# A hybrid residual layer in fp32 on one core: the opening sweep in seven stages, and GpSimd's exponent of its own

## The chip, the cores and the metric

The kernel runs on one core of a Trainium2 chip. The metric is the device time of one execution, in microseconds. Engines: TensorE (PE) multiplies matrices, VectorE (DVE) and ScalarE (ACT) work on elements, GpSimd (POOL) does small sums and issues some loads, and SyncE (SP) issues nearly all loads.

## The reference, cut to what matters

One layer over a sequence of 256 tokens of width 2048, all in fp32: an adaptive norm, a token mixer with one input projection, an output projection, a second norm, and a mixture of 32 experts. What the change touches is the head of it.

```python
ada = silu(c) @ w_ada + b_ada                     # w_ada: 2048 x 12288
sh_m, sc_m, gt_m, sh_f, sc_f, gt_f = split(ada, 6)
h = rms_norm(x, g_pre_mix) * (1 + sc_m) + sh_m    # x: 256 x 2048
proj = h @ w_in                                   # w_in: 2048 x 6160
...
x = x + gt_m * rms_norm(y, g_post_mix)
h = rms_norm(x, g_pre_ffn) * (1 + sc_f) + sh_f
y = hier_moe(h, ...)                              # 32 experts, w1, w3, w2
x = x + gt_f * rms_norm(y, g_post_ffn)
```

## The kernel before

The width of 2048 is 16 chunks of 128 columns. To project chunk k of h, the kernel needs 128 columns of the shift and of the scale, and each of these is a product of silu(c) with 2048 rows of w_ada. The opening sweep does both side by side, in stages of a few chunks. STAGES says which chunks are in which stage: before, six stages of 2, 3, 3, 3, 3 and 2.

**Loads.** SyncE's queue loads for each stage first its columns of w_ada, in pieces (4 rows to a partition for a stage of two chunks, 2 rows for one of three, `rows_of`), for shift and scale separately. One row of a piece is 128 columns times the chunks of the stage, which is 1,024 bytes for two chunks and 1,536 for three. A chunk of w_ada is 2.10 MB in all. Eight pieces fit in; for the ninth SyncE waits until the first is used up (`piece_done`). Then it loads the stage's rows of w_in, 2,560 columns (8,192 bytes and 2,048 bytes a row, 1.31 MB a chunk). There are homes for 8 chunks of w_in, so a stage's load waits until the stage is over (`stage_ps`) that used the home before. Behind the sweep stand the first two further units of w_in, 4 MB each, which wait for the last pieces, and the other columns of w_ada.

**VectorE.** `early(j)` multiplies and adds the sixteen rows of w_ada of stage j (L1208 for the first, L1210 for the others), transposes (L1221) and reduces (L1223) into `sums`. Between the pieces it also makes the additions of the stage before. TensorE has ten units of output columns to do in a stage, in the order of TURN. Six are held in PSUM banks over all stages. The other four, units 6 to 9, share one bank: when TensorE has ended one, VectorE adds it to its home (`added`, L1193 in the first stage, L1196 later), and only then may TensorE start the next of the four. ADDED_AT says behind which piece each addition comes, and unit 9's comes after the reduction:

```python
TURN = [6, 0, 7, 1, 8, 2, 3, 4, 9, 5]
ADDED_AT = {8: {1: 6, 3: 7, 5: 8}, 4: {0: 6, 2: 7, 3: 8}}   # pieces in a stage: {piece: unit}
...
if j and n_ in ADDED_AT[len(pieces(j))]:
    added(j - 1, ADDED_AT[len(pieces(j))][n_])
```

So VectorE is a stage ahead of TensorE: while TensorE does stage j, VectorE does the rows of stage j+1 and the additions of stage j.

**TensorE.** It first transposes x by two diagonal matrices of the inverse norms (L681). Before the ninth unit of a stage it folds the next stage's sums (L687), which needs them finished. The units' matmuls are at L717 (units 0 to 7) and L710 (units 8 and 9, against 512 columns). ScalarE takes the folded sums, forms shift and scale of each chunk (L1729, L1730) and applies them to the transposed x (L1734); the next stage's first unit waits for that.

**The first norms.** ScalarE squares both halves of x (L1714), GpSimd turns the sums into inverse roots (`rms`, L1976 and a power at L1979), and ScalarE makes the diagonals (L1719). The power's exponent, -0.5, is a column of the constants, whose second part (323 KB) is loaded last on ScalarE's queue; GpSimd waits for that part (`const_in[1]`).

Behind the sweep come two blocks of the projection, the other units with attention beside them, the output projection, routing, and the experts, whose weights are loaded into a ring of five places as matmuls free them.

Of the kernel before, what the change touches and what calls it, by code (L numbers as in the profile page):

```python
# [26 lines left out]
D = 2048  # L27
# [24 lines left out]
C_ID, C_LT, C_SUF, C_ONE, C_IOTA, C_NH, C_HALF, C_FOLD, C_FLIP, C_PAIR, C_BKT = 0, 128, 256, 384, 512, 544, 548, 550, 582, 710, 774  # L52
# [9 lines left out]
FIN_DVE = [(0, 0), (0, 1), (1, 0), (1, 1), (1, 2)]  # L62
FIN_PE = [(0, 2), (0, 3), (1, 3)]
X1T_BANK = [[2, 3, 4, 5], [6, 7, 0, 1]]
STAGES = [(0, 2), (2, 5), (5, 8), (8, 11), (11, 14), (14, 16)]
HOMES = 8
EARLY = 8
WIDE = 10
# [12 lines left out]

def rows_of(j):

    return {2: 4, 3: 2, 4: 2}[STAGES[j][1] - STAGES[j][0]]


def pieces(j):

    before = sum(KD // rows_of(i) for i in range(j))
    return [(before + i, rows_of(j) * i, rows_of(j) * (i + 1)) for i in range(KD // rows_of(j))]  # L90


PIECES = sum(KD // rows_of(j) for j in range(len(STAGES)))
HALF_PIECE = 2 * len(range(0, PIECES, 8)) + 1


def stage_of(k):

    return [lo <= k < hi for lo, hi in STAGES].index(True)


def slabs(j):

    lo, hi = STAGES[j]
    half = HOMES // 2
# [4 lines left out]
def wide_slabs(j):  # L110

    lo, hi = STAGES[j]
    cuts = [lo] + [k for k in range(lo + 1, hi) if k % HOMES in (0, 6)] + [hi]
# [106 lines left out]
def loads():  # L220

    out = [(4 * i + 3.9, ("unit", i + 3)) for i in range(7)]
    out += [(max(ada_slot(n - 4) + 0.5, 1.9), ("ada", n)) for n in range(4, 64)]
    return [("unit", 1), ("unit", 2), ("ada", 0), ("ada", 1), ("ada", 2), ("ada", 3)] + [item for _, item in sorted(out)]


def build(nc, a, out):
    f32, i32, u32 = mybir.dt.float32, mybir.dt.int32, mybir.dt.uint32
    ALU, ACT, AX = mybir.AluOpType, mybir.ActivationFunctionType, mybir.AxisListType
    SCHED = schedule()  # L230
    ctx = ExitStack()
    with ctx:
        def sb(name, shape, dt=f32):
            return ctx.enter_context(nc.sbuf_tensor(name, shape, dt))

        def sem(name):
            return ctx.enter_context(nc.semaphore(name))
# [9 lines left out]
        cst = sb("cst", [P, C_KEEP])  # L247
# [9 lines left out]
        st = sb("st", [P, 84])  # L257
# [126 lines left out]
        def piece(j, c):  # L384

            n = P * (STAGES[j][1] - STAGES[j][0])
            lo = UNIT // 4 * (c % 4)
# [3 lines left out]
        def unit_w(i):  # L391

            return slab(S1 if i % 2 else S0, 0, KD, 512)
# [23 lines left out]
        def ada_quarter(n):  # L417

            q = (n + 2) % 4
            return S2[:, D * q:D * q + D]  # L420
# [5 lines left out]
        c_in, tab_in, const_in, x_in, par_in, late_in = sem("c_in"), sem("tab_in"), [sem("const_in0"), sem("const_in1")], [sem("x_in0"), sem("x_in1")], sem("par_in"), sem("late_in")  # L426
        bias_in, rel_out = sem("bias_in"), sem("rel_out")
        unit_in = [sem(f"unit_in{i}") for i in range(2)]
        piece_in, piece_done = [sem(f"piece_in{n}") for n in range(8)], sem("piece_done")
# [6 lines left out]
        act_c, dve_c, pool_c = sem("act_chain"), sem("dve_chain"), sem("pool_chain")  # L436
        relrow_ps, relrow_sb = sem("relrow_ps"), sem("relrow_sb")
        small_exp, scale_sb = sem("small_exp"), sem("scale_sb")
        xsq, xr = sem("xsq"), sem("xr")
# [97 lines left out]
        def _(sp):  # L537
# [15 lines left out]
            for kind, i in loads():  # L553
                if kind == "unit":
                    if i == 1:
                        sp.wait_ge(piece_done, PIECES)
                    elif i == 2:
                        sp.wait_ge(piece_done, PIECES - 4)
                    elif i in (3, 4):
                        sp.wait_ge(blk_ps, 7 * (i - 2))  # L560
                    else:
                        sp.wait_ge(proj_ps, HELD + 2 * (i - 4))
                    if i < 8:
                        c = ORDER[4 + i]
                        sp.dma_start(unit_w(i), w_in[:, :, 512 * c:512 * c + 512]).then_inc(unit_in[i % 2], 16)
                    else:
                        u = i - 8
                        sp.dma_start(unit_w(i), w_out[:, :, 512 * u:512 * u + 512]).then_inc(unit_in[i % 2], 16)
                else:
                    if i in (0, 1):  # L570
                        sp.wait_ge(stage_ps, stage_of(11) + 1)
                    elif i >= 4:
                        sp.wait_ge(ada_done, i - 3)
                    sp.dma_start(ada_quarter(i), w_ada[:, i % KD, 2 + i // KD, :]).then_inc(ada_in[i % 4], 16)

            def first_load(n, w, js=(0, 1)):
                for j in js:
                    sp.dma_start(half(ring(n), j), half(w, j)).then_inc(ring_in[n % RING][j], 16)

            sp.wait_ge(ada_done, 64)  # L580
            sp.wait_ge(unit_in[1], 16 * 6)
            sp.wait_ge(piece_in[0], 16 * HALF_PIECE)
            first_load(1, w3[0])
# [87 lines left out]
        def _(pe):  # L671
# [72 lines left out]
            for item in SCHED:  # L744
# [11 lines left out]
                elif kind == "alpha":  # L756
# [12 lines left out]
                    else:  # L769
# [8 lines left out]
                        last.then_inc(suf_ps, 1)  # L778
                elif kind == "block":
                    _, b, part = item  # L780

                    def block_product(left, right, n):
# [30 lines left out]
                    else:  # L813
                        pe.wait_ge(blk_t, 4 * b + 8)
                        pe.wait_ge(blk_out, 8 * b + 2)
                        block_product(h_block(1, 1), quarter(b, 1, 0), 6)
                elif kind == "proj":
                    _, i, half, part = item
                    c = ORDER[i]
                    w, lo = unit_w(i - 4), 256 * half + P * part  # L820
# [15 lines left out]
                elif kind == "att":  # L836
# [26 lines left out]
                    if 1 <= i < ATT + 1:  # L863
                        j = i - 1
                        _, b = head_block(j)
                        pe.wait_ge(pd_sb, j + 1)
                        for kt in range(b + 1):
                            last = nc.tensor.transpose(bank(7)[:, P * kt:P * kt + P], pd[:, P * kt:P * kt + P], ident)
                        last.then_inc(pdT_ps, 1)
# [65 lines left out]
                elif kind == "prod":  # L935
# [11 lines left out]
                    elif p == 2:  # L947
                        pe.wait_ge(piece_in[0], 16 * HALF_PIECE)
                        pe.wait_ge(mix_sb, 4)
# [212 lines left out]
        def _(dve):  # L1162
# [185 lines left out]
            def sum_of(out_, in0, in1, n, op=ALU.add):  # L1348

                V.tensor_tensor(out_, in0, in1, op).then_inc(mix_sb, 1)  # L1350
                dve.wait_ge(mix_sb, n)
# [4 lines left out]
            def mix(name):  # L1356
# [18 lines left out]
                elif name == "T3":  # L1375
                    dve.wait_ge(piece_in[0], 16 * HALF_PIECE)
                    sum_of(T3, B22, B12, 7, ALU.subtract)
# [586 lines left out]
        def _(pool):  # L1964
            n_c = [0]
# [4 lines left out]
                n_c[0] += 1  # L1970
                pool.wait_ge(pool_c, n_c[0])

            def rms(src, dst, width):

                n = src.shape[1]
                nc.gpsimd.tensor_scalar(dst, src, 1.0 / width, EPS, ALU.mult, ALU.add).then_inc(pool_c, 1)  # L1976
                n_c[0] += 1
                pool.wait_ge(pool_c, n_c[0])
                return nc.gpsimd.tensor_tensor(dst, dst, cst[:, C_NH:C_NH + n], ALU.pow)  # L1979

            pool.wait_ge(const_in[1], 16)
            for t in range(TT):
                pool.wait_ge(xsq, t + 1)
                rms(st[:, t:t + 1], st[:, 2 + t:3 + t], D).then_inc(xr, 1)

            pool.memset(st[:, 82:83], EPS).then_inc(padded, 1)
            pool.memset(wrs[:, :], 0.0)
# [22 lines left out]
            for item in SCHED:  # L2010
# [16 lines left out]
                elif kind == "gsq":  # L2027
                    t = item[1]
# [42 lines left out]
```

## Time and profile before

| | |
|---|---|
| median of 3 runs (lowest, highest) | 1452.66 us (1451.88, 1452.72) |
| profiled execution | 1452.2 us, span 1450.3 us |
| TensorE busy | 1221.5 us (84%) |
| VectorE busy | 780.4 us (54%) |
| mean load rate over the span | 402 GB/s |
| mean granted clock of TensorE | 0.928 |
| chain that ended last | loads 42%, TensorE 33%, VectorE 3% |

The span is the time from the first to the last instruction; the shares of the chain say through what the last instruction can be followed back. Granted clock 1.00 is 2.4 GHz, 0.50 is 1.2 GHz, and a stretch's mean lies between. A line such as L1210 is that of the kernel's listing. In the timeline "x8" is eight like instructions merged, and the bracket tells how long the engine was idle ahead of them and what ended that.

### The profile page before, as it was taken

How to read it: one execution, taken by the hardware profiler on the slowest of the kernel's cores; microseconds unless marked ns; L12 is line 12 of the kernel's file. 1: busy time of each engine (PE TensorE's matmuls, PEld its weight loads, DVE VectorE, ACT ScalarE, POOL GpSimd, SP SyncE). 2: the span in 40 equal slices, each digit the busy share in tenths (PEclk: the TensorE clock that was granted, in tenths of full speed). 3: DMA queues.
4: the chain of work that ended last, by engine and by line, in shares of the span. 5: the costliest groups of instructions: out<-in, count | busy, mean ns of one | idle time of the engine just before them, and what ended most of it. 6: DMA issues, size and time to landing. Idle time of an engine off the chain costs nothing.

```text
span 1450.3 us, 18992 instructions
## 1 busy us (share of the span) xinstructions
PE 1221.5 (84%) x7437; PEld 573.8 (40%) x7438; DVE 780.4 (54%) x1106; ACT 210.4 (15%) x489; POOL 53.6 (4%) x76
## 2 busy tenths in 40 slices
PE   4899999999999989877776667767776679999967
PEld 3678788644444443222232222222222223333322
DVE  5777379897888765433343234323332335555525
ACT  3011131223111041000010001000000001111103
POOL 1000300020000020000000000000000000000020
PEclk9999999999999999888788789888888889999989
DMA  9999977999999899999999999999999999999996
GB/s 354 389 389 377 311 294 293 389 374 382 411 411 405 316 390 423 430 431 431 432 432 433 430 432 431 433 431 432 433 431 431 431 433 433 431 432 431 431 427 263
DMA packets 81653, 583.52 MB, mean 402 GB/s; under 512 B 5376, under 2 KB 30256, under 8 KB 56912
## 3 DMA queue, kind: packets, MB, share of 16 engines
q1 hardware_dynamic: 74256, 564.41, 94.4%
q10 hardware_dynamic: 5808, 14.85, 2.7%
q0 software_dynamic: 1552, 3.75, 0.9%
q8 instruction: 25, 0.41, 0.1%
q14 instruction: 12, 0.10, 0.0%
HBM read 579.30 MB, written 3.69 MB: 402 GB/s over the span
## 4 chain that ended last, share of the span: by engine, by line
DMA 42%; PE 33%; DVE 3%; issue 1%; ACT 1%; POOL 0%; SPq 0%; ACTq 0%; DVEq 0%
DMA stream<-in_w 41%; PE ps L1064 9%; PE ps L832 6%; PE ps L1120 4%; PE ps L1071 3%; PE ps L1020 2%; PE ps L923 2%; PE ps L1014 2%; DVE stream L1350 1%; PE ps L928 1%; PE ps L932 1%; DMA stream<-in_w_out 1%; PE ps L1026 0%; PE ps L890 0%; PE ps L900 0%
## 5 line engine op out<-in xcount | busy, mean ns | idle before, releaser
L1064 PE MATMUL ps<-stream,wk 128*32 128x512 f32 x2304 | 330.0, 711 | 178.8 <-DMA stream<-in_w 178.1
L1589 DVE TENSOR_TENSOR acc<-ps,acc 128x2048 f32<-128x2048 f32 x37 | 84.8, 2291 | 359.2 <-PE ps L1020 359.2
L1064 PEld LDWEIGHTS ps<-stream,wk 128*32 128x32 f32 x2304 | 74.7, 125 | 417.3 <-issue 329.9
L1120 PE MATMUL ps<-stream,cst 128*32 128x512 f32 x1152 | 131.5, 595 | 7.8 <-DMA stream<-in_w 7.8
L717 PE MATMUL ps<-stream 128*128 128x256 f32 x512 | 117.0, 388 | 6.3 <-DVE stream L1196 2.1
L832 PE MATMUL ps<-stream 128*128 128x512 f32 x256 | 112.7, 593 | 0.0
L717 PEld LDWEIGHTS ps<-stream 128*128 128x128 f32 x512 | 99.1, 194 | 26.9 <-issue 7.8
L1071 PEld LDWEIGHTS ps<-cst,wk 128*128 128x128 f32 x576 | 77.3, 209 | 69.7 <-issue 69.7
L1020 PE MATMUL ps<-wk,cst 32*128 32x512 f32 x592 | 92.1, 694 | 0.8 <-ACT wk L1929 0.8
L1210 DVE SCALAR_TENSOR_TENSOR wk<-stream,cc,wk 128x768 f32<-128x768 f32 (+1 forms) x90 | 83.5, 928 | 11.2 <-DMA stream<-in_w_ada 8.6
L1071 PE MATMUL ps<-cst,wk 128*128 128x32 f32 x576 | 85.5, 295 | 0.0
L1589 DVE TENSOR_TENSOR wk<-ps,wk 128x2048 f32<-128x2048 f32 x36 | 82.2, 2282 | 1.6 <-PE ps L1020 1.6
L1322 DVE SCALAR_TENSOR_TENSOR acc<-stream,cc,acc 128x2048 f32<-128x2048 f32 x30 | 70.4, 2348 | 10.0 <-DMA stream<-in_w_ada 8.9
L1637 DVE TENSOR_SCALAR cst<-cst 128x128 f32<-128x128 f32 x36 | 8.2, 228 | 116.3 <-ACT cst L1923 116.3
L1014 PE MATMUL ps<-resid,wrs 128*32 128x512 f32 x592 | 70.2, 592 | 0.2 <-DVE wrs L1576 0.2
L832 PEld LDWEIGHTS ps<-stream 128*128 128x128 f32 x256 | 47.5, 190 | 55.1 <-issue 55.1
L1120 PEld LDWEIGHTS ps<-stream,cst 128*32 128x32 f32 x1152 | 35.9, 109 | 77.7 <-issue 62.2
L1921 ACT ACTIVATE wk<-ps 128x512 f32<-128x512 f32 x36 | 21.5, 597 | 268.8 <-PE ps L1064 268.8
L965 PE MATMUL ps<-stream 128*128 128x512 f32 x112 | 48.6, 594 | 2.0 <-DMA stream<-in_w_out 2.0
L784 PE MATMUL ps<-stream 128*128 128x256 f32 x224 | 49.9, 381 | 0.3 <-PE ps L717 0.3
L1596 DVE COPY wk<-ps 128x256 f32<-128x256 f32 x74 | 27.9, 419 | 36.2 <-PE ps L1014 36.2
L784 PEld LDWEIGHTS ps<-stream 128*128 128x128 f32 x224 | 42.1, 190 | 7.1 <-issue 1.6
(291 smaller groups left out, 1151.9 us busy)
## 6 DMA issues: line engine op xcount, KB each, us to landing
stream<-in_w SPq DMA_DIRECT2D x87, 4096.0 KB, 41.8
stream<-in_w_ada SPq DMA_DIRECT2D x64, 1024.0 KB, 7.7
stream<-in_w SPq DMA_DIRECT2D x16, 2048.0 KB, 11.5
stream<-in_w_in SPq DMA_DIRECT2D x7, 4096.0 KB, 15.5
stream<-in_w_ada SPq DMA_DIRECT2D x64, 384.0 KB, 9.8
stream<-in_w_ada SPq DMA_DIRECT2D x16, 512.0 KB, 9.7
stream<-in_w_in SPq DMA_DIRECT2D x4, 2048.0 KB, 13.4
stream<-in_w_out SPq DMA_DIRECT2D x2, 4096.0 KB, 17.3
```

Source lines behind the costliest of these rows:

```text
L717: last = nc.tensor.matmul(bank(u if held else HELD, 2, S)[:, part, :], home(k, k + 1)[:, 0, 256 * u + P * part:256 * u + P * part + P], hT ...
L784: last = nc.tensor.matmul(block_bank(b, n), left[:, k, :], right[:, k, :], start=(k == 0), stop=(k == 7))
L832: last = nc.tensor.matmul(bank(fill % 2), hT[:, k, P * half:P * half + P], w[:, k, :], start=(k == 0), stop=(k == KD - 1))
L965: last = nc.tensor.matmul(bank(b), left[:, k, :], right[:, k, :], start=(k == 0), stop=(k == 7))
L1014: last = nc.tensor.matmul(bank(0)[32 * g:32 * g + 32, :], pick[:, t2, :], rows(t2)[:, g:KD:4, :], start=(t2 == 0), stop=(t2 == TT - 1))
L1020: last = nc.tensor.matmul(ps[:, b0 + g, :], spread[32 * g:32 * g + 32, t2, :], ye[32 * g:32 * g + 32, :], start=not onto, stop=True)
L1064: last = nc.tensor.matmul(bank(1 + m)[32 * g:32 * g + 32, :], xe[:, k + g, :], w13[m][:, k + g, :], start=(k == 0), stop=(k == KD - 4))
L1071: last = nc.tensor.matmul(bank(1 + m, 4, ROWS)[:, c, :], ab[m][:, P * c:P * c + P], cst[:, C_FOLD:C_FOLD + ROWS], start=True, stop=True)
L1120: last = nc.tensor.matmul(bank(2)[32 * g:32 * g + 32, :], hid[:, k, :], w2v[:, k, 512 * g:512 * g + 512], start=(k == 0), stop=(k == 3))
L1210: ins = V.scalar_tensor_tensor(out=out_, in0=w, scalar=cc[:, 2, k:k + 1], in1=out_, op0=ALU.mult, op1=ALU.add)
L1322: V.scalar_tensor_tensor(out=acc_m, in0=w, scalar=col, in1=acc_m, op0=ALU.mult, op1=ALU.add).then_inc(ada_done, 1)
L1589: V.tensor_tensor(y4, ps[:, b0:b0 + 4, :], y4, ALU.add).then_inc(ysum_sb, 1)
```

## The change

The stages become seven, of 1, 2, 3, 3, 3, 2 and 2 chunks. A stage of one chunk loads pieces of 8 rows. The wait for the second further unit of w_in is computed from the pieces' places now. GpSimd writes the exponent -0.5 into a spare column of `st` itself and waits for the second part of the constants only after the two roots.

```diff
-STAGES = [(0, 2), (2, 5), (5, 8), (8, 11), (11, 14), (14, 16)]
+STAGES = [(0, 1), (1, 3), (3, 6), (6, 9), (9, 12), (12, 14), (14, 16)]
...
-    return {2: 4, 3: 2, 4: 2}[STAGES[j][1] - STAGES[j][0]]
+    return {1: 8, 2: 4, 3: 2}[STAGES[j][1] - STAGES[j][0]]
...
+FIRST_HOME_FREE = 1 + max(c for c in range(PIECES) if c % 8 < 4)
...
-                        sp.wait_ge(piece_done, PIECES - 4)
+                        sp.wait_ge(piece_done, FIRST_HOME_FREE)
...
-            def rms(src, dst, width):
+            def rms(src, dst, width, half=None):
...
-                return nc.gpsimd.tensor_tensor(dst, dst, cst[:, C_NH:C_NH + n], ALU.pow)
-
-            pool.wait_ge(const_in[1], 16)
+                return nc.gpsimd.tensor_tensor(dst, dst, cst[:, C_NH:C_NH + n] if half is None else half, ALU.pow)
+
+            nc.gpsimd.memset(st[:, 6:7], -0.5).then_inc(pool_c, 1)
+            n_c[0] += 1
             for t in range(TT):
                 pool.wait_ge(xsq, t + 1)
-                rms(st[:, t:t + 1], st[:, 2 + t:3 + t], D).then_inc(xr, 1)
+                rms(st[:, t:t + 1], st[:, 2 + t:3 + t], D, st[:, 6:7]).then_inc(xr, 1)
+            pool.wait_ge(const_in[1], 16)
```

## Rows read from the trace of the kernel before

**Rows 1.** The chain that ended last, in order: start us, length us, what
```profile
451.93 13.75 PE ps L932 x32
...
466.43 12.17 DMA stream<-in_w_out
...
621.23 42.13 DMA stream<-in_w
```

**Rows 2.** TensorE's waits, 60 to 540 us: total us, times, longest us
```profile
PE ps L717 <- DVE stream L1196: 2.1, 1, 2.1
```

**Rows 3.** Timeline, 0 to 31 us: start, us, engine, line, operation, form, [idle before]
```profile
14.71 1.91 ACT L1714 ACTIVATE stream<-resid 128x2048 f32<-128x2048 f32 x1 [1.59 <-DMA resid<-in_x]
...
16.16 1.08 POOL L1979 TENSOR_TENSOR st<-st,cst 128x1 f32<-128x1 f32 x1
...
17.36 0.40 ACT L1719 ACTIVATE acc<-cst,st 128x128 f32<-128x128 f32 x1 [0.65 <-POOL st L1979]
...
17.81 9.61 PE L681 MATMUL ps<-acc,resid 128*128 128x128 f32 x64 [5.79 <-ACT acc L1719]
...
27.56 0.25 PE L687 MATMUL ps<-sums,cst 128*32 128x4 f32 x8
...
28.09 0.35 ACT L1729 ACTIVATE mod<-ps,bada,gains 128x1 f32<-128x1 f32 x1
...
29.02 1.09 ACT L1734 ACTIVATE stream<-stream,mod 128x256 f32<-128x256 f32 x2
...
29.76 1.53 PE L717 MATMUL ps<-stream 128*128 128x256 f32 x6 [1.95 <-ACT stream L1734]
```

**Rows 4.** Timeline, 31 to 110 us: TensorE's first matmul behind each gap
```profile
35.47 5.41 PE L717 MATMUL ps<-stream 128*128 128x256 f32 x16 [2.02 <-DVE stream L1193]
...
51.36 0.25 PE L687 MATMUL ps<-sums,cst 128*32 128x6 f32 x8 [3.59 <-DVE sums L1223]
...
62.98 7.13 PE L717 MATMUL ps<-stream 128*128 128x256 f32 x24 [2.11 <-DVE stream L1196]
```

**Rows 5.** Timeline: one stage of three chunks, fold to fold
```profile
106.63 0.25 PE L687 MATMUL ps<-sums,cst 128*32 128x6 f32 x8
...
115.53 4.17 DVE L1210 SCALAR_TENSOR_TENSOR wk<-stream,cc,wk 128x768 f32<-128x768 f32 x4
...
131.09 0.95 DVE L1223 TENSOR_REDUCE sums<-acc 128x24 f32<-128x768 f32 x1
...
132.87 0.25 PE L687 MATMUL ps<-sums,cst 128*32 128x6 f32 x8
```

**Rows 6.** Timeline: the last two stages
```profile
137.65 0.49 DVE L1208 TENSOR_SCALAR wk<-stream,cc 128x512 f32<-128x512 f32 x1 [1.03 <-DMA stream<-in_w_ada]
...
141.77 6.25 DVE L1210 SCALAR_TENSOR_TENSOR wk<-stream,cc,wk 128x512 f32<-128x512 f32 x8
...
148.06 0.69 DVE L1196 TENSOR_TENSOR stream<-ps,stream 128x512 f32<-128x512 f32 x1
...
148.81 2.84 PE L710 MATMUL ps<-stream 128*128 128x512 f32 x6
...
159.35 0.24 PE L687 MATMUL ps<-sums,cst 128*32 128x4 f32 x8
...
164.99 13.10 SPq L574 DMA_DIRECT2D stream<-in_w_ada  x4
...
183.37 2.48 DVE L1254 TENSOR_TENSOR stream<-stream 128x1024 f32<-128x1024 f32 x2 [2.11 <-PEq L741]
```

**Rows 7.** Windows: busy us by engine, granted clock, DMA share, GB/s
```profile
35.00:40.00 5.00, 4.53 (x13) 3.68 (x14) 4.77 (x6) 0.00 (x0) 0.00 (x0) 0.66 1.06 374
...
46.00:50.00 4.00, 1.77 (x9) 1.21 (x7) 3.86 (x5) 0.00 (x0) 0.00 (x0) 1.00 1.02 424
...
60.00:65.00 5.00, 2.89 (x11) 2.06 (x10) 4.74 (x6) 0.00 (x0) 0.00 (x0) 0.84 1.06 373
...
134.00:142.00 8.00, 8.00 (x35) 6.28 (x34) 4.27 (x7) 2.06 (x6) 0.00 (x0) 1.00 1.10 349
```

## The prediction

> **What bounds the kernel now.** I read the chain that ended last first. It is matmuls, then waits on the expert weights [rows 1]: up to about 465 us TensorE sets the pace, behind that the loads, which are issued as matmuls free the ring. Then the waits of TensorE from 60 to 540 us [rows 2]: between the sweep and the last output-projection matmul it hardly waits. So a microsecond more or less in the sweep is one at the end. The change lies wholly in the sweep, so the rest is its timeline, [rows 3] to [rows 6], and the load rates [rows 7].
>
> The first projection matmul starts at 29.76 [rows 3]; the sweep is over at 183.37, when VectorE is released by TensorE's marker (L741) [rows 6]. A stage of three chunks takes 132.87 - 106.63 = 26.24 us from fold to fold [rows 5], so 8.75 us a chunk. A stage has ten units, so one unit costs 0.875 us for each chunk. Sixteen chunks are 140 us. What exceeds that is mostly three gaps at the start, 2.0, 3.6 and 2.1 us, each ended by VectorE [rows 4], and stretches at half clock around them [rows 7].
>
> VectorE is the second party. One row of w_ada costs it 6.25/8 = 0.78 us for two chunks [rows 6] and 4.17/4 = 1.04 for three [rows 5]; the first of a stage costs less (0.49 [rows 6]). Sixteen rows are 12.2 and 16.2 us. To a stage come four additions of 0.7 us for units 6 to 9, which share one bank, so that the next of them can't start before VectorE has emptied it, and two closing operations (about 1.4 us for two chunks, 2.0 for three, from the 0.95 in [rows 5]). The reader should see how tight this is: the sums of (11,14) end at 132.04 and TensorE folds them at 132.87 [rows 5].
>
> **GpSimd's exponent.** It removes the wait on the second part of the constants. GpSimd starts its first power at 16.16; the second Square ends at 16.62, its sum a little later, but ScalarE's diagonal starts only at 17.36 [rows 3]. With the exponent at hand the first root is done before that, so the diagonal comes at 16.7: 0.65 us gained, once. The extra memset lies in idle time.
>
> **The first stage.** It has one chunk. Its w_ada is half as much in front of x, so x may land earlier; between 0 and 1 us, I take 0.5. The transposes run at 9.6 us as before and so start near 16.7 and end near 26.3. VectorE's sixteen rows, now of 256 columns at some 0.5 us each (0.78 and 1.04 carried on downward), fit in beside them. ScalarE forms the shift and scale of two chunks between 28.09 and 29.02 [rows 3], 0.46 each, so one chunk less saves 0.46. First projection at 29.76 - 0.65 - 0.5 - 0.46, about 28.1.
>
> **Stage 0, one chunk.** A unit is 0.875. Unit 6 ends at 29.0, its addition at 29.9. ADDED_AT puts unit 7's addition behind the third piece of the next stage, (1,3), whose first piece is done by then. Two pieces, 8 rows x 0.78 = 6.2, and the addition 0.7: 36.8. TensorE had units 6, 0, 7, 1 done at 28.1 + 3.5 = 31.6 and can't start unit 8: **a gap of 5.2**. Then four units, to 40.3; VectorE has a piece 3.1, an addition 0.7 and the closing 1.4, to 42.0: gap 1.7. Fold 0.2 and unit 9 end at 43.1, its addition at 44.0.
>
> **Stage 1, two chunks.** VectorE's work for (3,6) is 16.2 + 3 x 0.7 + 2.0 = 20.3, to 64.3. TensorE has only eight units of 1.75 beside it, from 44.0, that is 14.0: it idles 6.3 in all. Fold, units 9 and 5 (3.7): the stage ends at 68.0 with three chunks done. Before, eight chunks are done at 106.63 + 0.2 + 5.25 = 112.1, so three at 112.1 - 43.75 = 68.35. Of the earlier start 0.35 us is left.
>
> **Stages 2 and 3**, like those of before: 52.5, to 120.5.
>
> **Stage 4.** Here the loads count. Before, the first piece of the last stage comes at 137.65, after 1.03 us of waiting for it [rows 6]. The same bytes are loaded in another cut. Rows of 1,536 bytes go at 373 GB/s, of 1,024 at 349, of 8,192 at 424 [rows 7]. One chunk is 2.10 MB of w_ada and 1.31 MB of w_in: 5.6 + 3.2 = 8.8 us. Piece one of (12,14) has two chunks less ahead of it, -17.6. Two chunks go in 1,024 bytes where they went in 1,536: 2 x 2.10 x (1/349 - 1/373), +0.8. One chunk goes in 512 bytes where it went in 1,024. No sweep row shows this. The step from 1,536 to 1,024 bytes is, in time for 512 bytes on one of 16 engines, 65.9 - 46.9 = 19 ns, which leaves about 9 ns a row as fixed cost; so 512 bytes take 28 ns, 293 GB/s, and the chunk 7.2 us for 6.0: +1.2. Bounds: 0, if such rows cost no more a byte, and 2.4, twice that. I take +0.9, since part of it runs beside x. Arrival: 137.65 - 17.6 + 0.8 + 0.9 = 121.75. VectorE: first piece 0.5 + 3 x 0.78 = 2.85, addition 0.7, two pieces 6.25, addition 0.7: 132.25 at the earliest, and unit 8 wants to start at 120.5 + 10.5 = 131.0. **Gap 1.25.** End 148.0.
>
> The Trainium skill, DMA: Bandwidth & Descriptors (Specifications), gives 512 B as the least transfer for line rate. The trace disagrees already at 1,024 bytes (349 GB/s, against 424 for long rows [rows 7]). By the rule the +0.8 and +0.9 are nothing, the gap goes, and the sum below is 2.0 instead of 3.3.
>
> **Stage 5, a two-chunk stage before a two-chunk one**, which the kernel before doesn't have: there a three-chunk stage covered the wait: unit 7's addition came at 148.06, and unit 8 followed at 148.81 [rows 6]. VectorE starts at 148.0 - 2.6 + 0.9 = 146.3; first piece to 149.15; unit 6 ends at 149.75, its addition at 150.65; two pieces 156.9; unit 7's addition 157.6. TensorE is at unit 8 at 148.0 + 7.0 = 155.0: **gap 2.6**. The stage ends at 148.0 + 17.5 + 0.2 + 2.6 = 168.3.
>
> **Stage 6** is (14,16) as before: 183.37 - 164.99 = 18.4 [rows 6]. End 186.7, against 183.37: **+3.3 us**.
>
> **What I cost at nothing.** The four further additions and the seventh fold are in the chains above. SP's queue issues 93 loads instead of 95 in the sweep (76 of w_ada for 80, 17 of w_in for 15). The two units of 4 MB behind PIECES are issued at the last piece, 157.6 + 3.1 = 160.7, where it was 148.06 + 0.7 + 3.1 = 151.9 [rows 6]; at 373 to 424 GB/s the first takes 10 to 11 us [rows 7] and is wanted at 186.7, so some 14 us cover the 9; without them each microsecond would pass to the first block. w_ada beyond the sweep, behind it in the queue, waits for chunk 11, which is done a stage earlier relative to the end: no loss. GpSimd's parameter loads hang on the last fold, 5 us later than now; they are small, and wanted behind the first block's products. w_in of (9,12) and of (14,16) waits for chunks 3 to 5 and 6 to 8, done at 94 and 121 us; the queue comes to them near 98 and 137.
>
> **The rivals.**
>
> (a) The half clock. TensorE's granted clock fell to 1.2 GHz behind the gaps of 2.0 and 2.1 us: 0.66 on average from 35 to 40, 0.84 from 60 to 65 [rows 4, 7]. The new gaps near 60 and 155 are as long. One such stretch costs 5 x 0.34 = 1.7 us of full clock; behind the last gap nothing takes it up, so +5.0: 1457.7. Against it: about the gap of 3.6 (TensorE is idle up to 51.36) the trace shows no such stretch; 46 to 50 is at 1.00 [rows 4, 7]. A stretch near 65 is mostly taken up by the gap of 1.25.
>
> (b) Short rows cost no more a byte than long ones. Then the first piece of (12,14) comes at 120.05, stage 4 has no gap, and the rest stands: +2.0, 1454.7. For it: nothing in the sweep is as short as 512 bytes, so it isn't excluded. Against it: the fall from 373 to 349 GB/s [rows 7]. This is what the Trainium skill's line in DMA: Bandwidth & Descriptors (Specifications) would make of it.
>
> (c) Faster: the matmuls' earlier start survives. That needs VectorE to clear unit 7 early enough, in stages 0 and 5, that the gaps come to no more than the three of before; then 1.65 us are kept: 1451.0. It decides when unit 8 of stage 0 starts by 33.6 us or so. For it: TensorE lags the last sums by over 5 us before (it folds at 159.35), so there is room at the end. Against it: the order of VectorE's operations is fixed, 6.2 us of rows lie ahead of that addition.
>
> (d) Nothing to be seen: the gaps are there, but half of 5 and 6 goes because x or pieces land earlier: +0 to +2, 1453.7.
>
> **How the numbers follow.** Forecast 0.50, (a) 0.15, (b) 0.10, (c) 0.11, (d) 0.14. The sum is against the profiled execution, 1452.2 us with a span of 1450.3; the median of the runs shown, 1452.66, is 0.5 over it, and on it the forecast is 1456.0. About 0.2%, 2.9 us, is what can be told from no change, and 3.3 is close to it: the forecast's own range is +2.0 to +5.0 (arrival and half of a slow stretch), of which a fifth lies below 2.9. Slower: 0.41 + 0.15 = 0.56; within: 0.09 + 0.10 + 0.14 = 0.33; faster 0.11. Range 1451.4 to 1459.2, from most of (c) to a second slow stretch.
>
> **What would show it.** Diagonal at 16.1 to 16.8, first projection near 28; a wait of TensorE on VectorE's addition of 4 to 5.5 us near 32, some 6 us of waits from 44 to 64, one of 2.6 near 155; fold period 26.2 between; the sweep's end at 186.7. Wrong if unit 8 of the first stage waits under 3 us, if the stage after (12,14) begins before 166, or if the sweep ends later and the span doesn't.

## The result, and the profile after

The changed kernel takes 1456.76 us (median of 8 runs, 1455.76 to 1460.32) against 1452.69 for the kernel before (8 runs beside it, 1451.88 to 1454.40): a ratio of 1.0031 [1.0020, 1.0042], 4.1 us slower. The forecast was 3.3 us slower.

The profiled execution of the changed kernel took 1456.2 us with a span of 1454.3 (before: 1452.2 and 1450.3). The timeline of the first stages, with the rows that answer to [rows 3] and [rows 4]; a line number of before is one higher here. Columns as there.

```profile
11.96 0.56 POOL L1980 TENSOR_TENSOR st<-st 128x1 f32<-128x1 f32 x1
12.85 1.91 ACT L1715 ACTIVATE stream<-resid 128x2048 f32<-128x2048 f32 x1 [1.25 <-DMA resid<-in_x]
...
14.88 0.40 ACT L1720 ACTIVATE acc<-cst,st 128x128 f32<-128x128 f32 x1
...
26.78 3.95 PE L718 MATMUL ps<-stream 128*128 128x256 f32 x16 [1.77 <-ACT stream L1735]
27.99 0.69 DVE L1194 COPY stream<-ps 128x512 f32<-128x512 f32 x1 [2.42 <-PE ps L718]
28.59 6.26 DVE L1211 SCALAR_TENSOR_TENSOR wk<-stream,cc,wk 128x512 f32<-128x512 f32 x8
...
34.88 0.69 DVE L1194 COPY stream<-ps 128x512 f32<-128x512 f32 x1
...
35.63 2.07 PE L711 MATMUL ps<-stream 128*128 128x512 f32 x2 [4.90 <-DVE stream L1194]
...
48.02 3.72 PE L718 MATMUL ps<-stream 128*128 128x256 f32 x16 [0.67 <-DVE stream L1197]
...
52.84 1.98 PE L711 MATMUL ps<-stream 128*128 128x512 f32 x4 [1.09 <-DVE stream L1197]
...
63.83 0.25 PE L688 MATMUL ps<-sums,cst 128*32 128x6 f32 x8 [3.83 <-DVE sums L1224]
```

Read it as a chain. TensorE's first projection starts at 26.78, 3.0 us before the old one. VectorE takes unit 6 out of the shared bank at 27.99, then does eight rows of w_ada (28.59 to 34.85) and only then unit 7 (34.88). Unit 8 wants that bank: TensorE stands for 4.90 us. On the next stage it stands again, 0.67 + 1.09 + 3.83 = 5.59 us, the last time for VectorE's sums.

The last two stages, beside [rows 6], and what comes behind the sweep:

```profile
90.05 0.25 PE L688 MATMUL ps<-sums,cst 128*32 128x6 f32 x8
...
121.53 0.49 DVE L1209 TENSOR_SCALAR wk<-stream,cc 128x512 f32<-128x512 f32 x1 [1.49 <-DMA stream<-in_w_ada]
...
157.84 1.98 PE L711 MATMUL ps<-stream 128*128 128x512 f32 x4 [2.56 <-DVE stream L1197]
...
160.83 4.30 SPq L566 DMA_DIRECT2D stream<-in_w_in  x2
...
187.23 2.48 DVE L1255 TENSOR_TENSOR stream<-stream 128x1024 f32<-128x1024 f32 x2 [2.10 <-PEq L742]
...
199.39 1.28 DVE L1321 TENSOR_SCALAR acc<-stream,cc 128x2048 f32<-128x2048 f32 x1 [3.54 <-DMA stream<-in_w_ada]
```

The sweep is over at 187.23 instead of 183.37, 3.86 later; the span is 4.0 longer. So the loss is made in the sweep and passes to the end whole: span less sweep end is 1267.1 here and 1266.9 before. The waits of TensorE from 60 to 540 us say the same (total us, times, longest us): in the kernel before the longest was 2.1 us [rows 2], and here the two longest are both waits of the sweep.

```profile
PE ps L688 <- DVE sums L1224: 3.8, 1, 3.8
PE ps L711 <- DVE stream L1197: 2.6, 1, 2.6
```

The windows, which answer to [rows 7], with the same columns (the third number from the end is the granted clock):

```profile
33.00:34.00 1.00, 0.00 (x0) 0.00 (x0) 0.96 (x2) 0.00 (x0) 0.00 (x0) 0.70 0.97 393
35.00:40.00 5.00, 4.37 (x8) 2.86 (x9) 4.82 (x8) 0.00 (x0) 0.00 (x0) 0.50 1.03 378
40.00:42.00 2.00, 2.00 (x16) 1.49 (x15) 0.66 (x1) 0.16 (x1) 0.00 (x0) 0.95 1.06 372
60.00:65.00 5.00, 1.17 (x11) 0.67 (x11) 3.58 (x4) 0.87 (x5) 0.00 (x0) 0.91 1.02 387
65.00:70.00 5.00, 5.00 (x16) 3.17 (x15) 2.24 (x3) 2.00 (x6) 0.00 (x0) 0.75 1.06 373
```

At 1.2 GHz (0.50) TensorE was from 33.4 to 40.2, which is 6.8 us: 0.6 us of the first row (1 - 0.70 = 0.30, and each microsecond at half clock takes 0.5), the stretch to 40, and 0.2 of the third. It was so again for 0.9 + 2.5 = 3.4 us, 64.1 to 67.5. Before, the same sum gives 3.4 us from the window 35 to 40 and 1.6 from 60 to 65 [rows 7]; with 1.8 of this window of the kernel before the second is 3.4 too:

```profile
65.00:70.00 5.00, 5.00 (x21) 4.25 (x20) 4.33 (x5) 0.00 (x0) 0.00 (x0) 0.82 1.08 379
```

In the changed kernel TensorE had stood idle since 30.7 when the clock fell at 33.4, and from 60.0 to 63.8 ahead of the second fall.

The difference of 3.86 us, put together: the first projection 2.98 earlier; TensorE's gaps 4.90 + 0.67 + 1.09 + 3.83 + 2.56 = 13.05 for 2.02 + 3.59 + 2.11 = 7.72 before [rows 4], so +5.33; one fold more, 0.25; and the clock. Of the half-clock time, 4.6 us (35.6 to 40.2) and 3.4 us fell on a busy TensorE, 8.0 for 6.8 before, which is 0.6 us of full-clock work. Sum +3.2; the other 0.7 us I haven't traced.

The same 3.86 us can be split by place, at the fold of (6,9) at 90.05. There the changed kernel has done 5.4 chunks: three whole ones and eight of ten units of the next three. The kernel before has done 7.4 at its fold at 106.63 [rows 5]; less two chunks of 8.75 us, that is 89.1. So by then the start's 3.0 us are given back and 0.9 more. From there to the sweep's end are 97.2 us here and 183.37 - 89.1 = 94.2 before: the other 2.95, nearly all of it the gap of 2.56 and the further fold.

### The profile page after: what moved, and what is told of

It reads as the page before. It is cut to its first block, busy times and chain, and to the rows that moved or that the text cites. A ratio compares the mean times of both kernels' runs of the same rounds, so it can differ in the third digit from the quotient of the medians.

```text
span 1454.3 us, 19029 instructions
## 1 busy us (share of the span) xinstructions
PE 1218.8 (84%) x7445; PEld 572.0 (39%) x7446; DVE 786.1 (54%) x1128; ACT 210.3 (14%) x489; POOL 54.6 (4%) x77
## 3 DMA queue, kind: packets, MB, share of 16 engines
q0 software_dynamic: 1552, 3.75, 0.9%
## 4 chain that ended last, share of the span: by engine, by line
DMA 43%; PE 34%; DVE 1%; issue 1%; ACT 0%; POOL 0%; ACTq 0%; SPq 0%; DVEq 0%
DMA stream<-in_w 41%; PE ps L1065 9%; PE ps L833 6%; PE ps L1121 4%; PE ps L966 3%; PE ps L1072 2%; PE ps L1021 2%; DMA stream<-in_w_out 2%; PE ps L924 2%; PE ps L1015 2%; PE ps L1027 0%; PE ps L891 0%; PE ps L901 0%; PE ps L1139 0%; PE ps L861 0%
## 5 line engine op out<-in xcount | busy, mean ns | idle before, releaser
L1211 DVE SCALAR_TENSOR_TENSOR wk<-stream,cc,wk 128x768 f32<-128x768 f32 (+2 forms) x105 | 86.8, 827 | 9.5 <-DMA stream<-in_w_ada 6.3
L1597 DVE COPY wk<-ps 128x256 f32<-128x256 f32 x74 | 27.9, 419 | 33.5 <-PE ps L1015 33.5
## 6 DMA issues: line engine op xcount, KB each, us to landing
stream<-in_w_in SPq DMA_DIRECT2D x5, 2048.0 KB, 13.1
stream<-in_w_out SPq DMA_DIRECT2D x2, 4096.0 KB, 17.1
```

Source lines behind the costliest of these rows:

```text
L1211: ins = V.scalar_tensor_tensor(out=out_, in0=w, scalar=cc[:, 2, k:k + 1], in1=out_, op0=ALU.mult, op1=ALU.add)
```

## The experiments

Twelve runs were made, in four groups: eleven other kernels, and the changed kernel once more. Those of one group ran on one chip beside the kernel before. "Sweep end" is where VectorE is released by TensorE's marker, "rest" the span less that, both from the profile. The kernel before: 183.4 and 1266.9; the changed kernel: 187.2 and 1267.1.

| group: kernel | median us | ratio to before [95%] | first projection | sweep end | rest |
|---|---|---|---|---|---|
| 1: exponent_only | 1453.49 | 1.0000 [0.9992, 1.0009] | 29.0 | 182.5 | 1267.0 |
| 1: stages_only | 1457.26 | 1.0028 [1.0017, 1.0039] | 27.3 | 187.9 | 1267.4 |
| 1: order_first | 1459.31 | 1.0047 [1.0031, 1.0063] | 27.0 | 187.9 | 1267.3 |
| 1: order_last | 1458.66 | 1.0035 [1.0023, 1.0047] | 28.3 | 186.7 | 1270.2 |
| 2: order_all | 1460.38 | 1.0044 [1.0031, 1.0057] | 27.2 | 188.0 | 1270.6 |
| 2: order_all_ada_first | 1456.03 | 1.0023 [1.0014, 1.0032] | 26.9 | 186.8 | 1266.9 |
| 2: ada_first | 1457.95 | 1.0029 [1.0017, 1.0041] | 27.9 | 188.3 | 1268.9 |
| 2: pairs_at_end | 1462.53 | 1.0067 [1.0053, 1.0080] | 29.3 | 192.2 | 1267.7 |
| 3: pairs_at_start | 1461.51 | 1.0053 [1.0040, 1.0067] | 29.3 | 192.7 | 1266.1 |
| 3: six_order_exponent | 1451.64 | 0.9985 [0.9976, 0.9994] | 29.7 | 181.7 | 1269.3 |
| 4: changed_again | 1458.83 | 1.0041 [1.0028, 1.0054] | 28.1 | 189.1 | 1267.6 |
| 4: order_last_ada_first | 1456.18 | 1.0028 [1.0019, 1.0038] | 27.9 | 186.5 | 1267.1 |

The kernel before had medians of 1453.82, 1453.3, 1453.96 and 1452.84 in the four groups.

### The two parts apart

exponent_only is the changed kernel with the six stages of before:

```
-STAGES = [(0, 1), (1, 3), (3, 6), (6, 9), (9, 12), (12, 14), (14, 16)]
+STAGES = [(0, 2), (2, 5), (5, 8), (8, 11), (11, 14), (14, 16)]
```

> Kernel before with GpSimd's own exponent and the six stages. Theory (VectorE's chain and the arrival of w_ada set the early stages): the first projection comes 1.5 to 3 us earlier than 29.76, but VectorE still waits for the first piece of (2,5) at 30.4, so the fold of the second stage stays near 51.4 and the sweep's end near 183.4: 0 us, between -0.5 and +0.5. Rival (the start counts): the whole shift stays, -1.5 to -2.5 us.

stages_only keeps the seven stages and has the old power and the old wait:

```
-            nc.gpsimd.memset(st[:, 6:7], -0.5).then_inc(pool_c, 1)
-            n_c[0] += 1
+            pool.wait_ge(const_in[1], 16)
...
-                rms(st[:, t:t + 1], st[:, 2 + t:3 + t], D, st[:, 6:7]).then_inc(xr, 1)
-            pool.wait_ge(const_in[1], 16)
+                rms(st[:, t:t + 1], st[:, 2 + t:3 + t], D).then_inc(xr, 1)
```

> Changed kernel with the old wait for the constants. Theory: with a first stage of one chunk VectorE's chain hangs on unit 6 of stage 0, so the exponent is worth something here, but stage 4 waits for w_ada anyway: 0 to +1 us against the changed kernel, that is +4 to +5 against the kernel before. Rival (the exponent costs): +2 or less against the kernel before.

The exponent alone is worth nothing that can be told, 1.0000; the stages alone cost 1.0028, all of the change within the interval. Both times came as the theory had them, and 2 us or less for stages_only is outside its interval. The timeline of exponent_only shows where the earlier start goes:

```profile
29.04 5.38 PE L718 MATMUL ps<-stream 128*128 128x256 f32 x16 [1.81 <-ACT stream L1735]
...
29.98 0.62 DVE L1209 TENSOR_SCALAR wk<-stream,cc 128x768 f32<-128x768 f32 x1 [3.10 <-DMA stream<-in_w_ada]
...
51.23 0.29 PE L688 MATMUL ps<-sums,cst 128*32 128x6 f32 x8 [3.83 <-DVE sums L1224]
```

The projection starts 0.72 us earlier than at 29.76 [rows 3], not the 1.5 to 3 us that I expected. VectorE waits 3.10 us for its next piece whatever TensorE does, and the fold comes at 51.23, where it was 51.36 [rows 4].

stages_only has the old wait, and GpSimd's power from the constants:

```profile
14.56 0.56 POOL L1980 TENSOR_TENSOR st<-st,cst 128x1 f32<-128x1 f32 x1
...
15.24 0.40 ACT L1720 ACTIVATE acc<-cst,st 128x128 f32<-128x128 f32 x1
```

Its diagonal follows the second Square (13.17 to 15.08) without a wait for GpSimd, where the kernel before waited 0.65 us [rows 3]. With the smaller first load the constants land early enough, so in the changed kernel the exponent has next to nothing left to remove.

### Unit 7's addition one piece earlier: the first gap and the last

If the order of VectorE's work is what costs, then adding unit 7 behind the second piece instead of the third must take a gap away. order_first does so in the second stage alone, order_last in the last stage alone:

```
+                    at = {0: 6, 1: 7, 3: 8} if j == 1 else ADDED_AT.get(len(pieces(j)))
-                    if j and n_ in ADDED_AT[len(pieces(j))]:
-                        added(j - 1, ADDED_AT[len(pieces(j))][n_])
+                    if j and n_ in at:
+                        added(j - 1, at[n_])
```

(in order_last the condition is `j == len(STAGES) - 1`)

> Changed kernel with unit 7's addition one piece earlier in the second stage alone. TensorE's gap of 4.9 us near 31 shrinks to about 2. Theory: VectorE's total up to the fold is the same, and what is gained by TensorE is waited at the fold: 0 to -0.5 us against the changed kernel (+3.5 to +4 against before). Rival (the first gap is what costs): -3 us against the changed kernel, about +1 against before.

> Changed kernel with unit 7's addition one piece earlier in the last stage alone. The gap of 2.56 us before unit 8 near 155 goes; some of it comes back at the fold. Theory: -1.9 to -2.6 us against the changed kernel, +1.5 to +2.2 against before. Rival (the gap is filled by another wait, or the end is set elsewhere): unchanged, +4 against before.

The timeline of order_first:

```profile
32.73 1.13 PE L711 MATMUL ps<-stream 128*128 128x512 f32 x2 [1.75 <-DVE stream L1194]
...
41.06 0.29 PE L688 MATMUL ps<-sums,cst 128*32 128x4 f32 x8 [4.61 <-DVE sums L1225]
```

The gap at unit 8 shrinks from 4.90 to 1.75, and 4.61 us come up at the fold, where none had been. The fold is at 41.06, for 41.53. So at the start it isn't the order: VectorE's whole work for (1,3), sixteen rows, four additions and the sums, lasts longer than the eight units of one chunk that TensorE has beside it. The rival, that the first gap is what costs, forecast +1 against the kernel before, and the run is at 1.0047 [1.0031, 1.0063]. That is also more than the +3.5 to +4 of the theory; its sweep ends like that of stages_only and doesn't show why.

The timeline of order_last, at the other end:

```profile
164.42 0.25 PE L688 MATMUL ps<-sums,cst 128*32 128x4 f32 x8 [0.83 <-DVE sums L1225]
...
186.72 2.49 DVE L1256 TENSOR_TENSOR stream<-stream 128x1024 f32<-128x1024 f32 x2 [2.11 <-PEq L742]
...
202.24 1.29 DVE L1322 TENSOR_SCALAR acc<-stream,cc 128x2048 f32<-128x2048 f32 x1 [6.90 <-DMA stream<-in_w_ada]
...
205.78 7.17 PE L785 MATMUL ps<-stream 128*128 128x256 f32 x32 [1.06 <-DVE stream L1270]
```

There it is the order: the 2.56 us are gone and 0.83 is left at the fold. But the kernel wasn't faster than the changed one, against what I expected. The last two lines show a wait I hadn't counted: VectorE stands 6.90 us for a piece of w_ada behind the sweep, and TensorE twice about 1.06 for VectorE. "Rest" is 1270.2 instead of 1267.1, so more than the gap's gain is given back there (ratio 1.0035, the changed kernel's is 1.0031). TensorE's two waits are 2.1 of these 3.1 us; the other 1.0 isn't traced.

### The loads behind the sweep

SP's queue issues the two units of 4 MB at the last piece (160.83 in the changed kernel) and w_ada of the time behind the sweep after them. Theory: these rows of w_ada come too late as soon as the sweep ends earlier. The rival: the waits come from the additions' order itself. order_all has the new order in every stage of four pieces, order_all_ada_first also the issue order, and ada_first only this:

```
-ADDED_AT = {8: {1: 6, 3: 7, 5: 8}, 4: {0: 6, 2: 7, 3: 8}}
+ADDED_AT = {8: {1: 6, 3: 7, 5: 8}, 4: {0: 6, 1: 7, 3: 8}}
...
-    return [("unit", 1), ("unit", 2), ("ada", 0), ("ada", 1), ("ada", 2), ("ada", 3)] + [item for _, item in sorted(out)]
+    return [("ada", 0), ("ada", 1), ("ada", 2), ("ada", 3), ("unit", 1), ("unit", 2)] + [item for _, item in sorted(out)]
```

> Changed kernel with unit 7's addition one piece earlier in every stage of four pieces. By the arithmetic of the sweep alone its end moves from 187.2 to about 184.3, -2.9 us, and the time would be +1 against the kernel before. New theory, from the last-stage run: what follows the sweep is bound by loads issued at the last piece (two units of w_in, then w_ada for the next column group). VectorE then waits 7 to 9 us for the first of these w_ada loads, and TensorE some 2 to 3 us for VectorE, so most of the gain is given back: +2.5 to +4.5 against before.

> As the run with unit 7's addition earlier everywhere, and the four w_ada loads behind the sweep are issued ahead of the two units of w_in, which lets them start when chunk 11 is done (near 148) while the load engines are idle. New theory: VectorE's wait for w_ada behind the sweep and TensorE's waits behind that are gone, and the sweep's 2.9 us are kept: +0.5 to +1.5 against before. Rival (the sweep's end is all that matters): same time as without the other issue order. Rival (the units of w_in now come too late): a wait at the first block, +4 or more.

> Changed kernel with only the issue order of the loads behind the sweep changed, w_ada ahead of the two units. In the changed kernel VectorE waited 3.5 us for that load and TensorE did not wait for VectorE. Theory: nothing, +3.5 to +4.5 against before, as the changed kernel. If that wait does cost something further on, this run is 0.5 us or more faster than the changed kernel.

order_all repeats the finding, but it was a miss in size: 7.1 us over the kernel before, where I had +2.5 to +4.5. Its sweep ended at 188.0 instead of 184.3. The clock was at half for 17.1 us in it, for 10.2 in the changed kernel, which is up to 3.4 us of full-clock work. Its timeline behind the sweep:

```profile
203.36 1.29 DVE L1321 TENSOR_SCALAR acc<-stream,cc 128x2048 f32<-128x2048 f32 x1 [6.75 <-DMA stream<-in_w_ada]
...
206.91 7.17 PE L785 MATMUL ps<-stream 128*128 128x256 f32 x32 [0.90 <-DVE stream L1269]
```

In order_all_ada_first neither wait is there and "rest" is 1266.9: the theory on these waits holds. Its gain over order_all in one group is 1460.38 - 1456.03 = 4.4 us (in the two profiles 3.7 in the rest and 1.2 in the sweep). It still came out slower than I had expected, 1.0023 [1.0014, 1.0032]: the sweep ended at 186.8 where 184.3 was worked out. Its clock was at half for 6.8 us from 39.7 on and for 6.8 us more from 63.6 on, where the changed kernel had 6.8 and 3.4. ada_first is like the changed kernel, 1.0029. In the changed kernel VectorE's wait of 3.54 us is followed by none of TensorE, and ada_first, in which VectorE doesn't wait there, gains nothing. Its rest of 1268.9 is nearly 2 us above the others, and no wait that I can name stands for that. Its profile is of the slowest of its six runs, 1.2 us over their median, so part of this is that one execution.

order_last_ada_first joins the order of the last stage to that of the loads, and ran beside the changed kernel itself:

> The changed kernel once more, for a second profile of it beside the next run. Theory: the gaps that come from the order of work are the same to 0.1 us (about 4 to 5 near 31, 1.1 near 52, 3.8 at the fold near 64, 2.56 near 158), while the start (first projection 26.8 to 28.3) and the half-clock stretches near 30 to 47 and 64 to 72 differ from execution to execution and move the sweep's end by up to 2 us about 187.2.

> Changed kernel with unit 7's addition one piece earlier in the last stage alone and w_ada ahead of the two units behind the sweep. Theory: the last gap goes (-1.8 at the sweep's end) and nothing is given back behind it: no wait of VectorE of 3 us or more for w_ada near 196, no wait of TensorE on VectorE there, and 1.0 to 2.5 us less than the changed kernel in the same call, about +2 against before. Rival: as the run without the other issue order, +4 to +5.

Their timelines, changed_again first:

```profile
37.17 2.07 PE L711 MATMUL ps<-stream 128*128 128x512 f32 x2 [3.72 <-DVE stream L1194]
...
159.71 1.98 PE L711 MATMUL ps<-stream 128*128 128x512 f32 x4 [2.56 <-DVE stream L1197]
...
189.10 2.48 DVE L1255 TENSOR_TENSOR stream<-stream 128x1024 f32<-128x1024 f32 x2 [2.10 <-PEq L742]
```

and order_last_ada_first:

```profile
164.15 0.24 PE L688 MATMUL ps<-sums,cst 128*32 128x4 f32 x8 [0.83 <-DVE sums L1225]
...
186.45 2.48 DVE L1256 TENSOR_TENSOR stream<-stream 128x1024 f32<-128x1024 f32 x2 [2.11 <-PEq L742]
```

The sweep ends 2.65 us earlier and the median is 2.65 us lower (1456.18 against 1458.83). That the two agree so well is chance: from the fold of (6,9), the one at 90.05 in the first profile, to the sweep's end it is 95.3 us for 97.2, so 1.9 is what the last stages give, of which 1.73 is the gap (2.56 - 0.83). The other 0.7 comes ahead of it, where changed_again had half clock for 3.4 us more. VectorE's wait for w_ada behind the sweep (3.75 us in changed_again) is gone. The kernel is still 1.0028 [1.0019, 1.0038], since the loss ahead of that fold is untouched.

changed_again also shows how far the same program varies. The gaps are those of the first profile, 3.72 for 4.90, then 0.67, 1.09, 3.83 and 2.56, but the first projection starts at 28.07 instead of 26.78, and its windows give half clock for 3.4, 6.8 and 3.4 us:

```profile
28.00:34.00 6.00, 5.38 (x16) 4.14 (x16) 4.33 (x6) 0.00 (x0) 0.00 (x0) 0.72 1.08 392
...
35.00:44.00 9.00, 6.83 (x23) 4.56 (x24) 6.95 (x10) 0.28 (x2) 0.00 (x0) 0.62 1.05 376
65.00:70.00 5.00, 4.29 (x15) 2.30 (x16) 1.27 (x3) 2.87 (x9) 0.00 (x0) 0.66 1.06 374
```

(0.28 x 6, 0.38 x 9 and 0.34 x 5, each over 0.5.) The sweep ends 1.9 us later than in the other profile. So a difference under 2 us between single profiles of two kernels says little; the gaps behind the first, equal to 0.01 us in every kernel with these stages and this order, say much. All of the 1.9 lies ahead of the fold of (6,9), which comes at 91.92 for 90.05. Behind it all five profiles with these stages and the old order in the last one (order_first too) have 97.2 us, 2.95 more than before. Ahead of it they lose 0.9 to 2.8 us against before. So the pair at the end is a fixed part of the loss, and the start is one that varies, smaller in most of these profiles and about as large in changed_again.

### More stages of two chunks

If a two-chunk stage before a two-chunk stage costs 2.56 us by itself, then more of them cost more. pairs_at_end has four at the end, pairs_at_start two behind the first stage:

```
+STAGES = [(0, 2), (2, 5), (5, 8), (8, 10), (10, 12), (12, 14), (14, 16)]    # pairs_at_end
+STAGES = [(0, 1), (1, 3), (3, 5), (5, 8), (8, 11), (11, 14), (14, 16)]      # pairs_at_start
```

> Stages of 2, 3, 3, 2, 2, 2, 2 chunks with GpSimd's exponent: three times a stage of two chunks ahead of one of two. Theory: three gaps of 2.6 us before unit 8, and folds of 0.2 more: the sweep ends 7.5 to 8.5 us later than before, near 191, and the time is +8 to +10. Rival (only the first, one-chunk stage and its short rows cost): 0 to +1.

> Changed kernel with stages of 1, 2, 2, 3, 3, 3, 2: the same seven stages, the same one-chunk start, but the two pairs that follow each other lie early, and the last four stages are those of the kernel before. Theory: unit 8's gap before the last stage (2.56 us) is gone, the early gaps stay and are partly covered by the arrival of w_ada; the sweep ends near 185.1 to 186.2, +1.7 to +2.8 against before, and 1 to 2 less than the changed kernel. Rival (the one-chunk start is the whole cost): +4, as the changed kernel. Rival (the pair at the end is the whole cost): 0.

The timeline of pairs_at_end:

```profile
120.48 3.43 PE L711 MATMUL ps<-stream 128*128 128x512 f32 x4 [2.56 <-DVE stream L1197]
...
142.37 1.98 PE L711 MATMUL ps<-stream 128*128 128x512 f32 x4 [2.56 <-DVE stream L1197]
...
162.81 1.98 PE L711 MATMUL ps<-stream 128*128 128x512 f32 x4 [2.56 <-DVE stream L1197]
```

Three such borders, three gaps of 2.56. The first is also followed by half clock: four matmuls last 3.43 us where the two others last 1.98. The loss of 9.2 us (1462.53 less 1453.3) is what the theory gave.

pairs_at_start was a miss: I had the sweep end at 185.1 to 186.2, and it came at 192.7. Its timeline:

```profile
29.31 5.38 PE L718 MATMUL ps<-stream 128*128 128x256 f32 x16 [1.77 <-ACT stream L1735]
...
56.45 3.21 PE L711 MATMUL ps<-stream 128*128 128x512 f32 x4 [3.18 <-DVE stream L1197]
...
88.40 0.29 PE L688 MATMUL ps<-sums,cst 128*32 128x6 f32 x8 [3.83 <-DVE sums L1224]
```

The start was 2.5 us later than in the changed kernel, the new border cost 3.18 instead of 2.56, and the windows show four stretches at half clock, 3.4 + 3.4 + 3.4 + 6.8 = 17.0 us, of which the changed kernel has 10.2. Its gaps come to 12.1 us, less than the 13.1 of the changed kernel: it is the start (2.5 us) and the clock (up to some 4 us) that make the sweep end 5.4 later. So this run doesn't show that pairs cost more at the start than at the end, nor less; it shows that without a pair at the end the kernel can lose as much.

### A version that beats both kernels

six_order_exponent has the six stages of before, the exponent of the change and unit 7's addition one piece earlier:

> The six stages of before, GpSimd's exponent, and unit 7's addition one piece earlier in the last stage. In the exponent's run TensorE waited 0.7 us there and its sweep ended at 182.5 in place of 183.4. Theory: that 0.7 goes too, the sweep ends near 181.9, 0.8 to 1.5 us faster than before, unless a longer stretch at half clock takes it. Rival (all of it is covered by loads further on): 0.

1451.64 us, 0.9985 [0.9976, 0.9994]: 2.3 us faster than the kernel before in its group, and clear of the changed kernel, whose ratio to before is 1.0031 and 1.0041. It isn't clear of exponent_only, which ran in another group at 1.0000 [0.9992, 1.0009], so that the moved addition gains by itself is argued from the timeline (its 0.7 us gap in the last stage is gone). Its timeline has no wait of TensorE between the fold at 51.14 and the sweep's end:

```profile
51.14 0.29 PE L688 MATMUL ps<-sums,cst 128*32 128x6 f32 x8 [3.83 <-DVE sums L1224]
...
181.69 2.48 DVE L1255 TENSOR_TENSOR stream<-stream 128x1024 f32<-128x1024 f32 x2 [2.10 <-PEq L742]
```

1.7 us of the sweep are saved for 183.37; its rest, 1269.3, is 2.4 above that of before and hides part of it in the profile. That profile is of the slowest of its eleven runs, 1.2 us over their median, so half of the 2.4 can be that execution; the rest is open.

## Why the prediction was right

The forecast step by step against the first profile:

| step | forecast | measured |
|---|---|---|
| first projection | 28.1 | 26.78 |
| gap at unit 8 of stage 0 | 5.2 | 4.90 |
| fold behind it (gap) | 42.0 (1.7) | 41.53 (none over 0.5) |
| TensorE's gaps, stage 1 | 6.3 | 5.59 |
| fold of (3,6) | 64.3 | 63.83 |
| fold of (6,9) | 89.0 (from the steps) | 90.05 |
| first piece of (12,14) | 121.75 | 121.53 |
| gap in stage 4 | 1.25 | 0.24, as before |
| unit 8 of stage 5 (gap) | 157.6 (2.6) | 157.84 (2.56) |
| last piece, big units issued | 160.7 | 160.83 |
| sweep end | 186.7 | 187.23 |
| median | +3.3 | +4.1 |

**The mechanism held.** A smaller first stage starts TensorE earlier, and VectorE, whose operations come in a fixed order, gives it back twice; the two parts apart and the moved additions show it. One thing about it was put too narrowly. I spoke of the first gap as one of order. order_first shows that with another order the same time is lost at the fold (1.75 + 4.61 for 4.90): it is VectorE's amount of work against one chunk of TensorE's. How much of what the start loses (0.9 to 2.8 us by the fold of (6,9)) is that work, and how much the half clock behind the gaps, no run separates. In the last gap the order is the cause, as said (order_last, pairs_at_end).

**The start was mis-sized, without effect.** ScalarE's second Square, released by x, starts at 12.85 for 14.71 [rows 3]: x lands 1.9 us earlier where I had 0.5. The diagonal came at 14.88 instead of 16.1 to 16.8. GpSimd's exponent, 0.65 in my sum, has no such share in it (stages_only, above). The 1.3 us more bring the copy of unit 6 forward by 1.0, and with it VectorE's chain (its sums end at 40.66, forecast 42.0). But TensorE, at half clock from 33.4 to 40.2, isn't at the fold before 41.53, and half a microsecond remains.

**The gap of stage 4 was mis-sized.** From fold to fold it is 142.77 - 116.29 = 26.48 for a full stage of 26.24, so 0.24, not 1.25. The kernel before has the same 26.48 in its last stage of three, 159.35 - 132.87 [rows 5, 6], so stage 4 is no part of the difference. The piece arrived when I said; TensorE was late, and VectorE waited 0.21 us for its unit 6 there, not TensorE for the piece. From the fold at 63.83 to the next at 90.05 are 26.2 us, where my steps have 3.7 + 21.0 = 24.7. The 1.5 are the stretch at half clock from 64.1 to 67.5, which I had put into rival (a) as "mostly taken up by the gap of 1.25", and so it was in this execution: 1.05 late at 90.05, and level with my steps at 142.77 (142.75). That the sweep's end then came within 0.6 us owes something to luck. My steps have 0.35 us of the early start left at the fold of (6,9); the five profiles with these stages and the old order in the last one have lost 0.9 to 2.8 there, and the first profile is the one with the least.

**"w_ada beyond the sweep: no loss"** was right in time and wrong in the view. VectorE does wait 3.54 us for it, as it didn't before; TensorE has slack there in the changed kernel (ada_first: nothing gained), and has none once the last stage is 1.7 us shorter (order_last, order_all: some 3 us lost).

**The rivals.** (a) Half clock behind the last gap: not in this execution; the clock is full from 67.5 to the sweep's end. pairs_at_end has it behind one of its three such gaps, and the other four kernels or executions with this gap don't have it, so it is one in eight; the chance of 0.15 was no bad one. What I missed is that the early stretches are of varying length (3.4 or 6.8 us) and number (two or three); together with the varying start they moved the sweep's end by 1.9 us between two executions of one program. (b) Short rows at the price of long ones: the piece would have come at 120.05, and came at 121.53, and rows of 512 bytes went at 291 GB/s (last section), as I had worked out (293). That is also against the value of 512 B for line rate in the Trainium skill, DMA: Bandwidth & Descriptors (Specifications), for this stream. (c) Decided by unit 8 before 33.6: it came at 35.63, and even in order_first, where it came at 32.73, the fold took the time back; so (c)'s own criterion was wrong. (d) The gaps are there in full.

**Open.** Why the stretches at half clock are now 3.4, now 6.8 us behind like gaps; why the first projection starts anywhere from 26.8 to 29.3 in kernels with the same first stage (half of an answer is in the traces: the second Square, and so x, comes at 12.85 to 14.76, and the 64 transposes behind it take 9.0 to 10.4 us, since TensorE does 6 or 7 of them in a microsecond at first and 11 or 12 from some point between 19 and 23 us on; why either varies isn't shown); the 2 us of "rest" in ada_first and six_order_exponent; and why order_first, with a sweep that ends where that of stages_only does, has a median 2 us higher (1459.31 and 1457.26, one profile of each at 1457.0 and 1457.2).

## What to carry to other kernels

When the stages of a software pipeline are cut anew, compare, stage by stage, the second engine's whole work for the next stage with the first engine's time in this one: here a short stage ahead of a longer one lost more there than the early start had gained. Where two short stages meet, look at which operation in the second engine's fixed order frees a shared buffer, and move that one before resizing anything. And after shortening the end of a phase, look at the loads that are issued by its last step: they had been given time by the gap that was removed.

## What the runs showed of the hardware that was not expected

GpSimd's power of one column takes 0.55 or 0.56 us where VectorE stands idle beside it, and 0.73 to 1.08 us where VectorE is at work, whichever tile the exponent comes from. In the kernel before it takes 1.08 at 16.16 [rows 3], with VectorE at its rows from 16.07 on. stages_only has the same operation, with the exponent in the constants, at 0.56 (14.56, above), with VectorE idle up to 16.88. exponent_only has the exponent in its own tile, and its second power takes 1.06 beside VectorE's rows:

```profile
15.06 3.12 DVE L1211 SCALAR_TENSOR_TENSOR wk<-stream,cc,wk 128x512 f32<-128x512 f32 x4 [5.07 <-DMA stream<-in_w_ada]
...
17.52 1.06 POOL L1980 TENSOR_TENSOR st<-st 128x1 f32<-128x1 f32 x1
```

No run was made for this alone; it is read from where the two engines' work lies in time. In the changed kernel the first root is done at 12.52, well ahead of the diagonal, so this has no part in the time.

Rows of 512 bytes cost what was estimated. Two windows of the changed kernel, both of loads:

```profile
14.00:15.00 1.00, 0.00 (x0) 0.00 (x0) 0.00 (x0) 0.97 (x3) 0.07 (x1) 1.00 1.20 291
...
116.00:122.00 6.00, 6.00 (x30) 3.92 (x29) 1.16 (x2) 2.88 (x9) 0.00 (x0) 1.00 1.09 353
```

From 14 to 15 us nothing but w_ada's rows of 512 bytes is moved (570 packets, 0.29 MB): 291 GB/s, where the estimate had 293. Rows of 1,024 bytes go at 353 here and went at 349 before [rows 7].
